# Hybrid decoder layer on one core: another order for the first weight slabs of the opening

## The reference, cut to what matters

```python
def rmsnorm(x, gain):
    xf = x.astype(jnp.float32)
    y = xf * lax.rsqrt(jnp.mean(xf * xf, axis=-1, keepdims=True) + RMS_EPS)
    return (y * gain.astype(jnp.float32)).astype(x.dtype)

def swiglu(x, w_gate, w_up, w_down):
    return (jax.nn.silu(x @ w_gate) * (x @ w_up)) @ w_down

x = x + 0.5 * swiglu(rmsnorm(x, p['ffn1_norm']), p['ffn1_w_gate'], p['ffn1_w_up'], p['ffn1_w_down'])
...
```

## Time and profile before

| | us |
|---|---|
| median of 3 runs | 2078.71 (2077.58 to 2079.99) |
| the profiled execution, its own time | 2081.41 |
| its span | 2079.6 |
| TensorE busy (99% of the span) | 2066.8 |
| VectorE busy (65%) | 1343.4 |
| ScalarE busy (47%) | 986.7 |
| GpSimd busy (22%) | 449.4 |

### The profile page before, as it was taken

One profiled execution on the slowest core, in us unless ns is written; L12 is line 12 of the kernel. 1 busy time (PEld: TensorE's weight loads), 2 busy tenths in 40 slices (PEclk: granted clock), 3 DMA queues, 4 the chain that ended last, 5 costly groups with the idle time before them and its releaser, 6 DMA issues.

```text
span 2079.6 us, 48839 instructions
## 1 busy us (share of the span) xinstructions
PE 2066.8 (99%) x19331; PEld 2050.3 (99%) x19331; DVE 1343.4 (65%) x1449; ACT 986.7 (47%) x1189; POOL 449.4 (22%) x510
## 2 busy tenths in 40 slices
PE   9999999999999999999999999999999999999999
PEld 9999999999999999999999999999999999999999
DVE  7567567775555767766768968665555555555555
ACT  6654344444444545654454365554443444434443
POOL 0686414420000206763304430110000000000000
PEclk9999999999999999999999999999999999999999
DMA  8987789997897788759959976679887888878974
GB/s 252 275 276 226 260 260 270 279 264 260 251 266 221 234 299 277 236 179 321 329 177 326 283 229 196 193 248 279 263 260 244 254 271 265 260 244 256 268 217 159
DMA packets 442478, 526.47 MB, mean 253 GB/s; under 512 B 41520, under 2 KB 423392, under 8 KB 439552
## 3 DMA queue, kind: packets, MB, share of 16 engines
q1 hardware_dynamic: 427184, 507.59, 78.7%
q0 software_dynamic: 3248, 11.62, 1.6%
q10 hardware_dynamic: 11936, 5.72, 1.4%
HBM read 506.75 MB, written 105.04 MB: 294 GB/s over the span
## 4 chain that ended last, share of the span: by engine, by line
PE 92%; DVE 3%; DMA 3%; POOL 1%; ACT 1%; issue 1%; SPq 0%; ACTq 0%; DVEq 0%; POOLq 0%
PE pa L1551 30%; PE pa L1556 29%; PE pa L1552 29%; DMA qb<-q_dram 2%; DVE w_lo L1063 1%; PE pb L1754 0%; DMA raw<-in_w_in 0%; DVE xg_lo L1080 0%; DMA raw<-in_ffn_w_up 0%; PE pb L1862 0%; PE pb L1892 0%; POOL silu_v L2175 0%; DMA out_kv_p<-k_rows 0%; ACT w_hi L665 0%; PE pa L1920 0%
## 5 line engine op out<-in xcount | busy, mean ns | idle before, releaser
L1063 DVE TENSOR_TENSOR w_lo<-raw,w_hi 128x1024 fp32r<-128x1024 f32 x735 | 930.5, 1279 | 510.5 <-ACT w_hi L665 505.7
L665 ACT ACTIVATE w_hi<-raw 128x1024 fp32r<-128x1024 f32 x735 | 767.1, 1054 | 664.1 <-PE pa L1556 552.1
L1551 PE MATMUL pa<-xg_hi,w_hi 128*128 128x264 f32 x3960 | 924.6, 278 | 0.0
L1552 PE MATMUL pa<-xg_lo,w_hi 128*128 128x264 f32 x3960 | 916.2, 276 | 0.0
L1551 PEld LDWEIGHTS pa<-xg_hi,w_hi 128*128 128x128 f32 x3960 | 748.4, 189 | 8.3 <-issue 6.3
L1552 PEld LDWEIGHTS pa<-xg_lo,w_hi 128*128 128x128 f32 x3960 | 748.6, 189 | 0.2
L1556 PE MATMUL pa<-xg_hi,w_lo 128*128 128x264 f32 x3960 | 526.5, 276 | 0.0
L1556 PEld LDWEIGHTS pa<-xg_hi,w_lo 128*128 128x128 f32 x3960 | 483.3, 189 | 0.0
L1551 PE MATMUL pa<-act_hi,w_hi 128*128 128x264 f32 x1632 | 378.4, 276 | 0.0
L1552 PE MATMUL pa<-act_lo,w_hi 128*128 128x264 f32 x1632 | 377.9, 276 | 0.0
L1552 PEld LDWEIGHTS pa<-act_lo,w_hi 128*128 128x128 f32 x1632 | 308.5, 189 | 0.0
(11 more groups left out here) (364 smaller groups left out, 1353.3 us busy)
## 6 DMA issues: line engine op xcount, KB each, us to landing
raw<-in_ffn_w_up SPq DMA_DIRECT2D x172, 512.0 KB, 6.3
raw<-in_ffn_w_gate SPq DMA_DIRECT2D x171, 512.0 KB, 5.1
out_kv_s<-in_cache_kv_w SPq DMA_DIRECT2D x165, 512.0 KB
raw<-in_ffn_w_down SPq DMA_DIRECT2D x160, 512.0 KB, 4.6
raw<-in_w_in SPq DMA_DIRECT2D x152, 512.0 KB, 5.6
raw<-in_w_out SPq DMA_DIRECT2D x32, 512.0 KB, 4.9
raw<-in_w_ssm_branch SPq DMA_DIRECT2D x16, 512.0 KB, 4.6
raw<-in_ffn_w_down SPq DMA_DIRECT2D x16, 384.0 KB, 4.0
```

Source lines behind the costliest of these rows:

```text
L665: act.activation(w_hi[:, slot], raw[:, slot], ACT.Copy).then_inc(hi_ready, 1)
L1063: dve.tensor_tensor(w_lo[:, slot], raw[:, slot], w_hi[:, slot].bitcast(f32), ALU.subtract).then_inc(lo_ready, 1)
L1551: pe.matmul(out, wh, in_order(hi), start=first, stop=False)
L1552: pe.matmul(out, wh, in_order(lo), start=False, stop=False)
```

## The change

Six things are moved or replaced, all in the first iteration of `up00` and ahead of it. The first half of slab 0 is rounded by VectorE with a copy, ahead of first_lo(0), and ScalarE's activation for it is gone. VectorE's wait for the second `vec_t` and its copy to `stat` move behind the second half's remainder. `turn_in(0)` moves ahead of the waits and of the matmul with `same_sample`, and 8 of the 10 `keep_warm` transposes behind that matmul are gone. `second_products` multiplies slab 1's high products, then issues turn_in(2) and (3), then the low products. `split_hi` and `split_lo` of slab 2 move ahead of the conversions of x columns 2 and 3. `third_products` multiplies slab 2 in two halves, each in the order w_hi·x_hi, w_lo·x_hi, w_hi·x_lo; turn_in(4) and (5) now stand behind it, and (6) and (7) behind slab 3. `first_products` takes the low weights ahead of x_lo in its first half, and those of the second half last.

```diff
@@ scalar
             first_hi(0)
-            act.wait_ge(half_loaded, 16)
-            first_split_hi(0, w0_hi)
             first_hi(1)
             act.wait_ge(slab_loaded[0], 16)
             first_split_hi(1, hi_ready)
             split_hi(PH["up00"], 0, 1)
+            split_hi(PH["up00"], 0, 2)
             first_hi(2)
             first_hi(3)
-            split_hi(PH["up00"], 0, 2)
@@ vector
             samples_in()
+            dve.wait_ge(half_loaded, 16)
+            dve.tensor_copy(w_hi[:, 0, 0:2], raw[:, 0, 0:2]).then_inc(w0_hi, 1)
+            first_split_lo(0, w0_hi, 1, w0_lo)
+            first_lo(0)
+            first_lo(1)
+            first_split_lo(1, hi_ready, 1, lo_ready)
             dve.wait_ge(vec_t, 2)
             dve.tensor_copy(stat[:, 14:15], pb[:, 3, KD:KD + 1]).then_inc(vec_ready, 1)
-            first_lo(0)
-            first_split_lo(0, w0_hi, 1, w0_lo)
-            first_lo(1)
-            first_split_lo(1, hi_ready, 1, lo_ready)
             split_lo(PH["up00"], 0, 1)
             x_out(0)
             x_out(1)
+            split_lo(PH["up00"], 0, 2)
             first_lo(2)
             first_lo(3)
-            split_lo(PH["up00"], 0, 2)
@@ tensor, first_products
+                    if half == 0:
+                        pe.wait_ge(w0_lo, 1)
+                        for c, kk in tiles_of:
+                            pe.matmul(pa[:, c, 0:T], w_lo[:, 0, kk, P * c:P * c + P], in_order(xg_hi[:, kk, :]), start=False, stop=False)
                     pe.wait_ge(xlo_ready, half + 1)
                     for c, kk in tiles_of:
                         pe.matmul(pa[:, c, 0:T], w_hi[:, 0, kk, P * c:P * c + P], in_order(xg_lo[:, kk, :]), start=False, stop=False)
-                    pe.wait_ge((w0_lo, lo_ready)[half], 1)
+                pe.wait_ge(lo_ready, 1)
+                for c, kk in tiles_of:
+                    ins = pe.matmul(pa[:, c, 0:T], w_lo[:, 0, kk, P * c:P * c + P], in_order(xg_hi[:, kk, :]), start=False, stop=False)
+                ins.then_inc(slab_used, 1)
+
+            def second_products(ph):
+
+                b = 2 * ph.banks(0, 1)
+                pe.wait_ge(hi_ready, 2)
+                for kk in range(KS):
+                    for c in range(2):
+                        high_products(pa[:, b + c, 0:T], 1, kk, P * c, xg_hi[:, kk, :], xg_lo[:, kk, :], kk == 0)
+                turn_in(2)
+                turn_in(3)
+                pe.wait_ge(lo_ready, 2)
+                for kk in range(KS):
+                    for c in range(2):
+                        ins = low_product(pa[:, b + c, 0:T], 1, kk, P * c, xg_hi[:, kk, :], False)
+                ins.then_inc(slab_used, 1)
+
+            def third_products(ph):
+
+                b = 2 * ph.banks(0, 0)
+                pe.wait_ge(hi_ready, 3)
+                for half in range(2):
+                    tiles_of = [(c, kk) for c in range(2) for kk in (2 * half, 2 * half + 1)]
+                    pe.wait_ge(xhi_ready, half + 3)
                     for c, kk in tiles_of:
-                        ins = pe.matmul(pa[:, c, 0:T], w_lo[:, 0, kk, P * c:P * c + P], in_order(xg_hi[:, kk, :]), start=False, stop=False)
+                        pe.matmul(pa[:, b + c, 0:T], w_hi[:, 2, kk, P * c:P * c + P], in_order(xg_hi[:, KS + kk, :]), start=False, stop=False)
+                    pe.wait_ge(lo_ready, 3)
+                    for c, kk in tiles_of:
+                        low_product(pa[:, b + c, 0:T], 2, kk, P * c, xg_hi[:, KS + kk, :], False)
+                    pe.wait_ge(xlo_ready, half + 3)
+                    for c, kk in tiles_of:
+                        ins = pe.matmul(pa[:, b + c, 0:T], w_hi[:, 2, kk, P * c:P * c + P], in_order(xg_lo[:, KS + kk, :]), start=False, stop=False)
                 ins.then_inc(slab_used, 1)
@@ tensor, up(i) of ffn
-                                if g == 0 and not (first and j == 0):
+                                if g == 0 and not (first and j in (0, 2)):
                                     pe.wait_ge(xlo_ready, 8 * xn + 2 * s + 2)
                                 if first and j == 0:
                                     first_products(ph)
+                                elif first and j == 1:
+                                    second_products(ph)
+                                elif first and j == 2:
+                                    third_products(ph)
                                 else:
                                     slab_products(ph, i, j, g, xg_hi, xg_lo, KS * s, KS, s == 0, s == 3)
-                                if first and j < 3:
-                                    turn_in(2 * j + 2)
-                                    turn_in(2 * j + 3)
+                                if first and j in (2, 3):
+                                    turn_in(2 * j)
+                                    turn_in(2 * j + 1)
@@ tensor, start
             pe.transpose(pa[:, 2, 0:P], x_rows[:, 2, 0:P], ident[:]).then_inc(xs_t, 1)
+            turn_in(0)
             pe.wait_ge(const_ready, 4)
             pe.wait_ge(sq_ready, 1)
             pe.wait_ge(vec_ready, 1)
             pe.matmul(pb[:, 3, KD:KD + 1], same_sample[:], stat[:, 15:16], start=True, stop=True).then_inc(vec_t, 1)
-            keep_warm(3)
-            turn_in(0)
-            keep_warm(3)
+            keep_warm(2)
             turn_in(1)
-            keep_warm(4)
             ffn(0)
```

## The result

The changed kernel takes 2080.61 us in the median of 22 runs (2079.28 to 2083.62), the kernel before 2078.16 us in the median of 22 runs beside them (2074.62 to 2081.08). The ratio is 1.0013, 95% interval 1.0008 to 1.0019: slower by 1.7 to 3.9 us, 2.5 by the medians. The forecast was 4.6 us more, 2083.3.

The account below looks back on a forecast made before the run. The prediction took TensorE's stream of matmuls as the bound, with the opening set by slab 0's end and ScalarE's queue to the root. 2.9 us for the later root plus 1.7 for the clock gave 4.6, 2083.3 us; range 2080.2 to 2085.6.

Parts of the forecast that it names:

- Slab 0: Opening: VectorE's copy, taken as 0.6 us, stays hidden, first_hi(1) starts as before, slab 0 ends 0.1 us earlier.
- 16 products ahead of the turning: Slab 1's high products stand before turn_in(2) and (3): 1.8 us, so first_hi(2) starts at 13.8 instead of 12.12.
- Up to rows_t 7: TensorE has 24 more instructions before rows_t 7, 2.7 us, plus 0.3 of idle in slab 2; it comes at 22.2.
- ScalarE's work up to the root: From first_hi(6) to the root ScalarE keeps 7.8 us of work without a hole; root at 30.0, 2.9 later.
- GpSimd's three instructions and line 1607 follow 2.9 later.: Behind the root, the pieces and the spread of rstd shift equally: line 1607 at 34.4 instead of 31.52.
- What is late next: Behind the spread, all later work was taken to hang on TensorE's progress, so the 2.9 us stays to the end.
- The clock after the gap: A 3.5 us TensorE gap before line 1607 lowers its clock, as near 1199 us: 1.7 us more; chance 0.33.
- rival (a): The gap before line 1607 doesn't lower the clock: 2.9 us alone, 2081.6; chance 0.22.
- (c): ScalarE is relieved in the opening, the root comes 1.2 us earlier or more: faster, 2077.5; chance 0.05.
- Rival (b): Opening's clock rises later, slab 0 ends 1.3 later: 2084.6 with the gap's loss (chance 0.22), 2082.9 without (0.13).

Follow-up runs that it names:

- nudge: The kernel before with one small 128x128 copy on VectorE that makes its subtraction of slab 7 start later; ratio to before 0.9998.
- late_spread: turns_back with the spread of rstd issued behind the first 12 high products of slab 7 instead of ahead of them; ratio to before 0.9999.
- turns_back: The changed kernel with the transposes of x back at their old places, behind slabs 0, 1 and 2; ratio to before 0.9996.
- squares_early: The changed kernel with the squares of x's first block of rows taken earlier on ScalarE, ahead of first_hi(4); ratio to before 1.0007.
- gap_long: The changed kernel with one more pass of squares, result unused, on ScalarE ahead of the root; ratio to before 1.0027.
- late_warm: late_spread with keep_warm(5) besides; ratio to before 0.9998.
- vector_busy: The changed kernel with four unused 128x528 subtractions on VectorE behind the reciprocal; not timed, distance between two marks 54.78 us against 50.26 in before.

## Why the forecast came out as it did, step by step

**Slab 0.** Right in its mechanism: turn_in(1) waited 0.39 for its columns and first_hi(1) started at 7.75, where it had. The copy took 0.43, not 0.6, under cover. The 0.1 us of gain can't be seen: slab 0 ended anywhere from 10.8 to 12.9 in ten profiles with the new opening and at 11.5, 11.5, 11.7 and 14.0 in four with the old one, depending on when x lands and when the products go from 0.22 to 0.11 us apart.

**16 products ahead of the turning.** Forecast 1.8; from the first mark first_hi(2) moved from 0.64 to 2.44: 1.8.

**Up to rows_t 7.** Forecast 2.7 + 0.3 = 3.0, measured 3.2. The term for slab 2's wait was 0.3 and should have been 0.5: TensorE waits at both xhi 3 and xlo 3.

**ScalarE's work up to the root.** Forecast unchanged at 7.8; 30.80 - 23.04 = 7.8.

**"GpSimd's three instructions and line 1607 follow 2.9 later."** The first step that failed. I took their 3.6 us from the one profile as a price. It was a price with a condition: by the time of the later root VectorE was free, the reciprocal came 0.33 behind the root's start and not 0.47, GpSimd's first piece came ahead of the subtraction by more than its own length, and the pieces gave 1.4 us back, 1.5 with the sooner start. nudge shows that in the kernel before itself.

**What is late next.** Missed: +0.75 for the gate values. VectorE's subtraction for slab 7 waits for the split that stands behind the root in ScalarE's queue, and two more subtractions and two copies follow before it reads the gate values at 36.84, though rstd is ready at 34.9. This wait comes with GpSimd's short pieces, not with the late root: nudge and late_spread, with roots as early as before's, have it (0.37 and 0.33), and turns_back and squares_early, with long pieces, have not. So the two steps together are a root 3.2 later less 0.75.

**The clock after the gap.** The second step that failed, and the largest: 1.7 us, none measured. With GpSimd's pieces shorter and TensorE later in its slabs the gap was 1.81 and not 3.5; and at 3.62 (gap_long) the clock held too. Here rival (a) was right: the granted clock read 1.00 in every stretch from 34 to 40 us.

Together 3.2 - 1.5 + 0.75 + 0 = 2.5, against a forecast of 2.9 + 1.7 = 4.6. The direction and its cause, the transposes behind other work, were right; a third of the size, 1.7 of 4.6, was a clock loss carried over from one gap elsewhere. That the time still fell into the stated range is partly luck. 2080.61 lies 0.4 above the lower edge, 2080.2, and for that edge the prediction gives no sum; every scenario that it priced except (c) gives 2081.6 or more. Part of the rest is the base: the three runs of before had a median of 2078.71, the 22 beside the changed kernel 2078.16. And of its chances the largest, 0.51, was on a time 0.2% or more above before, which didn't come. Rival (b), a later rise in the opening, happened in this profile (products 0.22 us apart until about 11 us), but also in nudge and late_warm, with ten and five warming transposes: the smaller number isn't shown to be its cause, and it stays open. The spacing is the only sign of it, since the granted clock reads 1.00 from 0 to 14 us in every profile, also where the products are 0.22 apart. Rival (c) never came near: ScalarE's hole filled with slab 2's split, but it got two more, of 0.73 and 2.00 us.

## What to carry to other kernels

Where one engine feeds a chain over three others, moving its small instructions behind its large ones makes the whole chain later, even if it was idle itself in neither place; look at what each moved piece releases before looking at what it waits for. When the executions scatter more than the effect, find two instructions that stand at fixed places of the order and compare their distance: it repeated to 0.05 us here where whole runs scattered by several. And before crediting a shorter wait to an edit, look whether an instruction beside it changed its time as well. And don't carry a duration of one engine into an order in which another engine's instruction, on the same memory, comes first.

## What the runs showed of the hardware

**A subtraction of VectorE holds up GpSimd's pieces, and 0.1 us of order decides which.** Two `TENSOR_SCALAR` of 128x128 on GpSimd took 1.9 to 2.3 us when a 128x1024 subtraction of VectorE started 0.16 to 0.58 behind the first, and 1.2 when it started 0.66 or more behind; then the subtraction was longer (1.30 to 1.38 against 1.23 to 1.28) and the 128x8 piece took 1.04. In the four profiles with long pieces the second piece ended 0.46 to 0.48 behind the end of the subtraction. The Trainium skill, "SBUF — State Buffer", section "SBUF: two separate sides", says that such a pair shares one set of ports, that the instruction that starts first keeps them to its end, and that the other is blocked. By that rule nudge should bring the short times, and it did. Other rows don't fit its "starts first" as they stand: in before the 128x8 piece started at 30.00, ahead of the next subtraction at 30.07, and took 1.38 where it took 0.53 in vector_busy, and in turns_back the subtraction that started 0.30 behind the first piece took 1.23, the same as in before. GpSimd's rows are rough, so this may be a matter of what a row's start means. I had not weighed the rule for the forecast.

**TensorE's clock.** A gap of 3.2 us near 1196 us was followed by the 1.2 GHz level in 13 of 14 profiles. At 31 us, gaps of 1.8 (five profiles) and 3.6 us (one) were followed by a granted clock of 1.00, one of 5.6 us by about 3.4 us at the low level. The Trainium skill, "TensorE: Matmul & The Clock Gate", Part 1, has the clock fall back when TensorE idles; the 13 profiles and the longest gap agree, but a gap's length alone did not tell whether it would.

**The scatter of the runs.** With the same order, x's second columns made TensorE wait 0 to 0.9 us, and the spacing of the opening's matmuls fell from 0.22 to 0.11 anywhere between about 8 and 13 us. Both move the end by as much as the whole change.
